# Two PSUM banks for the attention's projections, an earlier load of their weights, and another order of the prologue

## The reference

```python
def gdn_mixer(h, w_in, conv_w, a_log, dt_bias, out_norm, w_out):
    proj = h @ w_in                      # q, k, v | z | b | a
    ...
    beta = jax.nn.sigmoid(b)
    g = -jnp.exp(a_log) * jax.nn.softplus(a + dt_bias)
    o = gated_delta_rule_chunked(q, k, v, beta, g)
    ...
def mla_mixer(h, w_in, q_latent_norm, w_q_up, w_out, k_nope, k_rope, v, cos, sin):
    proj = h @ w_in
    c_q = rmsnorm(proj[..., :MLA_Q_RANK], q_latent_norm)
    z = proj[..., MLA_Q_RANK:]
    q = (c_q @ w_q_up).reshape(B, L, MLA_HEADS, MLA_QK)
    ...                                  # rope, causal softmax, times v
    return (o * jax.nn.silu(z)) @ w_out
```

## Time and profile before

| | us |
|---|---|
| median of 3 runs | 2503.44 (2501.28 to 2508.81) |
| the profiled execution's own time | 2494.57 |
| its span | 2492.8 |
| TensorE busy | 2286.7 (92%) |
| VectorE busy | 961.1 (39%) |
| ScalarE busy | 747.1 (30%) |
| mean granted clock | 0.951 |

### The profile page before, as it was taken

The page is one execution under the profiler, slowest core; times in us unless marked ns, Lnnn a source line. Parts: engine busy times, 40 slices in busy tenths (PEclk is TensorE's granted clock), DMA queues, the critical chain, the costliest instruction groups (busy, mean ns, idle before and its releaser), DMA issues.

```text
span 2492.8 us, 42870 instructions
## 1 busy us (share of the span) xinstructions
PE 2286.7 (92%) x19147; PEld 1651.8 (66%) x19147; DVE 961.1 (39%) x1821; ACT 747.1 (30%) x1376; POOL 0.2 (0%) x4
## 2 busy tenths in 40 slices
PE   4899999999998998788999999798999988999999
PEld 4678778878777687444444444356566546888888
DVE  1435535544544301222322220356226634556532
ACT  2434343343443201233433421442344422000000
POOL 0000000000000000000000000000000000000000
PEclk8899989989999799889998999899999998999999
DMA  4122222122121142111111112121110031433330
GB/s 160 35 69 71 68 69 70 52 87 70 52 70 52 49 118 68 30 30 30 30 46 57 37 34 68 55 70 36 35 34 1 1 101 34 131 85 89 94 101 26
DMA packets 200624, 150.41 MB, mean 60 GB/s; under 512 B 16360, under 2 KB 198122, under 8 KB 200058
## 3 DMA queue, kind: packets, MB, share of 16 engines
q1 hardware_dynamic: 200442, 147.69, 19.9%
HBM read 143.41 MB, written 4.26 MB: 59 GB/s over the span
## 4 chain that ended last, share of the span: by engine, by line
PE 85%; ACT 6%; DVE 5%; issue 3%; SPq 1%; DMA 1%; DVEq 0%; ACTq 0%
PE PS L2226 15%; PE PS L1505 11%; PE PS L1533 5%; PE PS L442 5%; PE PS L674 5%; PE PS L736 4%; PE PS L1286 3%; PE PS L1295 3%; PE PS L1288 3%; PE PS L1465 2%; PE PS L792 2%; PE PS L680 1%; PE PS L717 1%; PE PS L718 1%; PE PS L2347 1%
## 5 line engine op out<-in xcount | busy, mean ns | idle before, releaser
L2226 PE MATMUL PS<-hn_all,ring 128*128 128x264 f32 x1536 | 426.3, 414 | 2.5 <-DVE scr L2781 1.5
L2226 PEld LDWEIGHTS PS<-hn_all,ring 128*128 128x128 f32 x1536 | 292.5, 201 | 51.2 <-ACT scr L2551 1.9
L674 PE MATMUL PS<-hn_all,ring 128*128 128x512 f32 x256 | 117.0, 601 | 7.3 <-DMA ring<-in_mla_w_q_up 7.3
L442 PE MATMUL PS<-big,ring 128*128 128x264 f32 x512 | 115.8, 390 | 2.4 <-DMA ring<-in_gdn_w_out 2.4
L442 PEld LDWEIGHTS PS<-big,ring 128*128 128x128 f32 x512 | 98.3, 192 | 19.9 <-issue 2.7
L736 PE MATMUL PS<-big,ring 128*128 128x512 f32 x256 | 111.2, 592 | 0.0
L1286 PE MATMUL PS<-ring,hn_all 128*128 128x256 f32 x384 | 95.4, 403 | 2.5 <-ACT scr L1731 2.5
L1505 PE MATMUL PS<-scr 128*128 128x256 f32 x352 | 84.8, 384 | 4.6 <-DVE scr L1996 4.6
L674 PEld LDWEIGHTS PS<-hn_all,ring 128*128 128x128 f32 x256 | 48.2, 193 | 59.6 <-issue 47.5
L736 PEld LDWEIGHTS PS<-big,ring 128*128 128x128 f32 x256 | 48.2, 190 | 58.3 <-issue 57.7
L869 ACT ACTIVATE scr<-PS,scr 128x528 f32<-128x528 f32 (+1 forms) x64 | 34.6, 541 | 169.6 <-DVE scr L955 169.4
(11 more groups left out here) (471 smaller groups left out, 4043.1 us busy)
## 6 DMA issues: line engine op xcount, KB each, us to landing
ring<-in_w_mod SPq DMA_DIRECT2D x24, 1024.0 KB, 5.4
ring<-in_gdn_w_in SPq DMA_DIRECT2D x16, 1024.0 KB, 5.5
ring<-in_w_in SPq DMA_DIRECT2D x12, 1024.0 KB, 5.4
hn_all<-in_w_ffn_in SPq DMA_DIRECT2D x22, 512.0 KB, 5.3
ring<-in_w_ffn_in SPq DMA_DIRECT2D x22, 512.0 KB, 5.2
ring<-in_mla_w_in SPq DMA_DIRECT2D x9, 1024.0 KB, 5.5
ring<-in_gdn_w_in SPq DMA_DIRECT2D x16, 512.0 KB, 5.3
ring<-in_gdn_w_out SPq DMA_DIRECT2D x8, 1024.0 KB, 7.2
```

Of the source, the lines that this page charges most:

```text
L442: ins = nc.tensor.matmul(PS[:, 2 * (m % 2) + h, 0:x.stop - x.start], wslot(m % 4, P, 16)[:, k, :], src[:, k, x], start=(k == 0), stop=(k = ...
L674: ins = mm(o, wz_pair(p)[:, k, j * P:(j + 1) * P], hq[:, k, :], start=(k == 0), stop=(k == KD - 1))
L2226: ins = mm(o, wslot(slot_, 256)[:, k, m * P:(m + 1) * P], hn[:, k, b * HALF:(b + 1) * HALF], start=(k == 0), stop=(k == KD - 1))
```

## The change

Three things change. In the prologue the tokens are loaded and transposed ahead of the small vectors; `b` and `a` are computed with the 32 weight columns stationary and `hn` moving, one step as each block of `hn` is there, in four groups of 32 output partitions (L2229 after), and are folded and transposed into rows by six small matmuls (`gate_rows`); the projections start ahead of the gates, and the gates' work on TensorE, ScalarE and VectorE is put between them. In the first attention the weights of pair 0 are loaded once block 5 of the output product is done, and the latent's weights go to slots 2 and 3. The pieces alternate between banks 7 and 6, each waits only for the last eviction of its own bank, VectorE's rotation has a semaphore of its own, and the product with the values, which also uses bank 6, waits for the last piece there.

```diff
-    put("ident32", (i[:, None] % B32 == j[None, :]).astype(np.float32))
+    put("ident32", (np.arange(P)[:, None] % B32 == j[None, :]).astype(np.float32))
...
+        bap = scr[:, 14 * D + 512:14 * D + 512 + L]
...
+        def piece_bank(n):
+            h, kind = PIECES[n - 1]
+            if h == 0:
+                return 7 - (n - 1) % 2
+            return {"z": 7, "qn": 6, "qr": 7, "ka": 6, "kb": 7, "v0": 6, "v1": 7, "vm": 6}[kind]
+
+        def piece_before(n):
+            return max([k for k in range(1, n) if piece_bank(k) == piece_bank(n)], default=0)
...
         def mla_sp(sp):
-            sp.wait_ge(*up("gout", KD))
-            wd = t["kv_w_down"].rearrange("(k p) n -> p k n", p=P)
-            w = wslot(0, 256)
...
+            sp.wait_ge(*up("gout", 6))
+            weights(0)
+            sp.wait_ge(*up("gout", KD))
+            wd = t["kv_w_down"].rearrange("(k p) n -> p k n", p=P)
+            w = wslot(2, 256)
+            for o, src in ((w[:, :, 0:192], wd), (w[:, :, 192:224], wd[:, :, 160:192]), (w[:, :, 224:256], wd[:, :, P:160]),
+                           (wslot(3, 256), w_min[:, :, 0:256])):
+                sp.dma_start(o, src).then_inc(s["md_in"], 16)
+            sp.wait_ge(*up("md_mm", 4))
             weights(1)
-            sp.wait_ge(*up("md_mm", 4))
-            weights(0)
...
-                if n > 1 and part != 1:
-                    pe.wait_ge(*up("pev", n - 1))
-                o = PS[:, 7, :]
+                b_ = piece_bank(n)
+                last = piece_before(n)
+                if last and part != 1:
+                    if kind == "qn" and h >= 2:
+                        pe.wait_ge(*up("ogm", h - 1))
+                    elif PIECES[last - 1][1] == "qr":
+                        pe.wait_ge(*up("prot", evicted(last)[1]))
+                    else:
+                        pe.wait_ge(*up("pev", evicted(last)[0]))
+                o = PS[:, b_, :]
...
                     pe.wait_ge(*up("ogm", n))
+                if nxt:
+                    in6 = max(k for k, x in enumerate(PIECES) if x[0] == n + 1 and piece_bank(k + 1) == 6) + 1
+                    pe.wait_ge(*up("pev", evicted(in6)[0]))
...
-                V.tensor_tensor(qr_b[h % 2], PS[:, 7, :], rope[:, N_META:L], ALU.mult).then_inc(s["pev"], 1)
+                V.tensor_tensor(qr_b[h % 2], PS[:, piece_bank(piece_no(h, "qr")), :], rope[:, N_META:L], ALU.mult)\
+                    .then_inc(s["prot"], 1)
...
             sp.dma_start(CT[:, :], t["tables"]).then_inc(s["const_in"], 16)
+            sp.dma_start(min_, t["meta_tokens"]).then_inc(s["x_in"], 16)
+            for k in range(4):
+                sp.dma_start(xin[:, k, :], t["x"][0, k * P:(k + 1) * P, :]).then_inc(s["x_in"], 16)
...
-            sp.dma_start(min_, t["meta_tokens"]).then_inc(s["x_in"], 16)
...
+            pe.wait_ge(*up("vec_in", 16 * 24))
+            nc.tensor.transpose(PS[:, 0, 0:P], rows_a, ident)
...
-            pe.wait_ge(*up("hn0", 1))
-            for c in range(NCH):
-                for k in range(KD):
-                    ins = mm(PS[0:C, 0, 32 * c:32 * c + 32], hn[:, k, c * C:(c + 1) * C], wba[:, k, :],
-                             start=(k == 0), stop=(k == KD - 1))
+            for k in range(KD):
+                pe.wait_ge(*up("hn0", k + 1))
+                g = 32 * (k % 4)
+                for h in range(2):
+                    ins = mm(PS[g:g + 32, 4 + h, 0:HALF], wba[:, k, :], hn[:, k, h * HALF:(h + 1) * HALF], start=(k < 4),
+                             stop=(k >= 4))
             ins.then_inc(s["ba_mm"], 1)
...
+            def gate_rows():
+                pe.wait_ge(*up("act_g", 2))
+                pe.wait_ge(*up("vec_ev", 1))
+                for c in range(NCH):
+                    ins = mm(PS[0:C, 0, 32 * c:32 * c + 32], bap[:, c * C:(c + 1) * C], const("ident32"), start=True, stop=True)
+                ins.then_inc(s["ba_mm"], 1)
+
+            def gate_sums():
+                pe.wait_ge(*up("ba_ev", 1))
...
-            for name in ("qa", "qb", "ka", "kb", "v0a", "g0a", "g0b", "v0b", "g1a", "g1b"):
+            item("qa", 0)
+            gate_rows()
+            for name in ("qb", "ka"):
+                item(name, 0)
+            gate_sums()
+            for name in ("kb", "v0a", "g0a", "g0b", "v0b", "g1a", "g1b"):
                 item(name, 0)
...
-            for name in ("qa", "qb", "ka", "kb"):
-                raw(name, 0)
+            raw("qa", 0)
+            gates_a()
+            raw("qb", 0)
+            gates_b()
+            raw("ka", 0)
+            raw("kb", 0)
+            gates_c()
```

More of the change, by code:

```diff
@@ L167 @@
     "gla_r": ("ms0", 1), "gcopy": ("rev", 16), "gla_l": ("rr", 16), "lam_d": ("csil_z", 1),
-    "gsil": ("h_out", 16), "gfin": ("hn0", 1), "fs_d": ("mx", 64), "fp_d": ("pn", 64), "fv_d": ("pt", 64), "ft_d": ("tr", 64),
-    "op_d": ("sc", 64), "ov_d": ("ex", 64), "os_d": ("pj", 104), "ot_d": ("pev", 104), "lrl": ("rstd0", 1), "mo_t": ("go_t", 8),
+    "gsil": ("h_out", 16), "gfin": ("hn0", 8), "fs_d": ("mx", 64), "fp_d": ("pn", 64), "fv_d": ("pt", 64), "ft_d": ("tr", 64),
+    "op_d": ("sc", 64), "ov_d": ("ex", 64), "os_d": ("pj", 104), "ot_d": ("pev", 88), "prot": ("dve_g", 2), "lrl": ("rstd0", 1), "mo_t": ("go_t", 8),
 }
@@ L579, in piece_no, with evicted @@
             return PIECES.index((h, kind)) + 1
+        def evicted(n):
+            return n - sum(x[1] == "qr" for x in PIECES[:n]), sum(x[1] == "qr" for x in PIECES[:n])
+        def piece_bank(n):
[5 more added lines that the diff above has]
+            return max([k for k in range(1, n) if piece_bank(k) == piece_bank(n)], default=0)
         def last_piece(h):
@@ L744, in early @@
                     if m == 0:
-                        pe.wait_ge(*up("pev", len(PIECES)))
+                        pe.wait_ge(*up("pev", evicted(len(PIECES))[0]))
+                        pe.wait_ge(*up("prot", MLA_HEADS))
                     else:
@@ L751, in mla_pe @@
                 nxt = n + 1 < MLA_HEADS
-                pe.wait_ge(*up("pev", last_piece(n)))
+                pe.wait_ge(*up("pev", evicted(last_piece(n))[0]))
+                pe.wait_ge(*up("prot", n + 1))
                 score(n, 3)
@@ L846, in piece @@
                 act.wait_ge(*up("pj", piece_no(h, kind)))
+                b_ = piece_bank(piece_no(h, kind))
                 if kind == "z":
@@ L2101, in _ @@
             sp.dma_start(rows_c, t["gla_gate_bias_2"][0].rearrange("z (k p) -> (z k) p", p=P)).then_inc(s["vec_in"], 16)
-            sp.dma_start(min_, t["meta_tokens"]).then_inc(s["x_in"], 16)
-            for k in range(4):
-                sp.dma_start(xin[:, k, :], t["x"][0, k * P:(k + 1) * P, :]).then_inc(s["x_in"], 16)
             sp.dma_start(wba, w_gdn[:, :, GDN_BA:GDN_BA + 32]).then_inc(s["vec_in"], 16)
@@ L2482, in _ @@
                 A(sq0[:, k, :], hT[:, k, :], ACT.Square).then_inc(s["sq0_done"], 1)
-            act.wait_ge(*up("vec_ev", 1))
-            for n, name in enumerate(("c", "cctx")):
-                act.wait_ge(*up("csil_z", 1))
-                A(csil[:, n::32], cols(name), ACT.Silu).then_inc(s["c_act"], 1)
+            act.wait_ge(*up("vec_tr", 1))
+            A(vecs[:, 0:2 * P + 4], PS[:, 0, 0:2 * P + 4], ACT.Copy).then_inc(s["vec_ev"], 1)
             act.wait_ge(*up("ms0", 1))
@@ L2496, in _, with gates_a, gates_b, gates_c @@
             A(nega, alog, ACT.Exp).then_inc(s["act_g"], 1)
+            act.wait_ge(*up("vec_ev", 1))
+            for n, name in enumerate(("c", "cctx")):
+                act.wait_ge(*up("csil_z", 1))
+                A(csil[:, n::32], cols(name), ACT.Silu).then_inc(s["c_act"], 1)
             act.wait_ge(*up("ba_mm", 1))
-            A(g3[0], ba[:, :, 0:16], ACT.Exp, scale=-1.0).then_inc(s["act_g"], 1)
-            act.wait_ge(*up("dve_g", 1))
-            act_link(A(gx[3], gx[2], ACT.Exp))
-            A(gx[3], gx[3], ACT.Ln, bias=one[0:C]).then_inc(s["act_g"], 1)
-            act.wait_ge(*up("gate_gc", 1))
-            A(GV[:, 0:96], PS[0:C, 0, 0:96], ACT.Copy).then_inc(s["act_g"], 1)
-            A(gx[4], PS[0:C, 0, 0:96], ACT.Exp).then_inc(s["act_g"], 1)
-            act.wait_ge(*up("dve_g", 2))
-            A(gx[5], gx[5], ACT.Exp).then_inc(s["act_g"], 1)
+            A(two(bap), PS[:, 4:6, 0:HALF], ACT.Copy).then_inc(s["act_g"], 1)
+            def gates_a():
+                act.wait_ge(*up("ba_mm", 2))
+                A(g3[0], ba[:, :, 0:16], ACT.Exp, scale=-1.0).then_inc(s["act_g"], 1)
+            def gates_b():
+                act.wait_ge(*up("dve_g", 1))
+                act_link(A(gx[3], gx[2], ACT.Exp))
+                A(gx[3], gx[3], ACT.Ln, bias=one[0:C]).then_inc(s["act_g"], 1)
+            def gates_c():
+                act.wait_ge(*up("gate_gc", 1))
+                A(GV[:, 0:96], PS[0:C, 0, 0:96], ACT.Copy).then_inc(s["act_g"], 1)
+                A(gx[4], PS[0:C, 0, 0:96], ACT.Exp).then_inc(s["act_g"], 1)
+                act.wait_ge(*up("dve_g", 2))
```

(2 more changed lines are left out.)

50 lines of the change are left out of this document (20 added, 30 removed).

## The result

| | before | after |
|---|---|---|
| median, us | 2504.76 (2501.28 to 2508.81, 4 runs) | 2418.43 (2414.95 to 2422.33, 4 runs) |
| the profiled execution's own time | 2494.57 | 2422.33 |
| its span | 2492.8 | 2420.6 |
| TensorE busy | 2286.7 | 2265.0 |
| mean granted clock | 0.951 | 0.955 |

The ratio is 0.9656, 95% interval 0.9638 to 0.9674: 86.3 us by the medians, 72.2 by the two profiled executions. The forecast was 2427, within 2412 to 2455. Ratios are of the runs outside a slower state that a few executions fall into, so a ratio can differ by some tenths of a per cent from that of two medians.

The account below looks back on a forecast made before the run. TensorE fills 85% of the span, so gains lie where it idles or runs at half clock. 14.3 + 9.3 + 7.5 + 37 + 8 = 76.1 us; 76 off the runs' median 2503.44 gives 2427, range 2412 to 2455.

Parts of the forecast that it names:

- prologue, net: Prologue, measured by the start of `v0b`: 26.2 us gained less 11.9 given back, 14.3 us net, bounds 5 and 18.5.
- weights of pair 0: Start of the first attention: a 7.30 us DMA wait and 2.0 us of half clock in `z` go, 9.3 us.
- head 0's pieces: First attention: with two banks evictions lie beside the pieces, so the scores come sooner; 7.5 us taken.
- loop, waits of 15 iterations: Loop over heads: looser eviction waits gain 3.6 us in seven long iterations, 1.5 in eight short; 37 us.
- loop, clock: Loop over heads: half-clock stretches that follow the pieces' gaps mostly go; 8 us, bounds 0 and 9.1.
- Tokens first: Start of the prologue: `x` is issued earlier, so TensorE reaches the tokens at 12.0, 7.0 us earlier; bounds 5 to 8.
- the lower one: Prologue: lower bound, 0.9 us, for how far behind `hn` the matmuls of `b` and `a` end; 3.6 was taken.
- What is given back: Prologue, from `qa`'s end to `v0b`: gates now between projections cost 9.6 us, `v0b` at the half clock 2.3 more.
- The stall before `g0a`: Prologue, behind the projections: a sign that the forecast holds, a TensorE stall of about 4 us.
- That the prologue gives all back: Rival, 10%: gates, convolutions and SiLU become the prologue's chain; gain 0 to 5 us instead of 14, time 2438.
- That evictions bind the loop anyway: Rival, 5%: ScalarE's order holds each piece of the loop as before; gain 10 us there, time 2462.
- That many small waits make the clock fall in each iteration: Rival, 2%: two banks split the loop's waits into many small ones; 7 us lost, time 2510.

Follow-up runs that it names:

- e_balate: Kernel after, but the matmuls of `b` and `a` wait for all eight blocks of `hn`: 2416.59 us, ratio 0.9675.
- e_weights: Kernel before with only head pair 0's weights loaded earlier, during the output product: 2494.32 us, ratio 0.9978.
- e_banks: Kernel before with only the two alternating banks and their waits: 2445.60 us, ratio 0.9765.
- e_prologue: Kernel before with only the prologue's part of the change: 2480.19 us, ratio 0.9906.
- e_banks_serial: Kernel before with two banks, but each piece still waits for the eviction of the piece right in front: 2512.65 us, ratio 1.0054.
- e_vserial: Kernel after, but value pieces of heads behind the first wait for the eviction of the piece right in front: 2433.98 us, ratio 0.9755.
- e_zlate: Kernel after with head 0's first piece `z` put behind the norm's reductions: 2412.95 us, ratio 0.9666.
- both last edits: Kernel after with `z` behind the norm's reductions and the gates ahead of the raw keys: 2407.96 us, ratio 0.9644; run again 2405.03, 0.9615.

## Why the prediction was right, and where it was off

| step | predicted, us | by the profiles, us |
|---|---|---|
| prologue, net | 14.3 | 17.4 |
| weights of pair 0 | 9.3 | 9.3 |
| head 0's pieces | 7.5 | 7.3 |
| loop, waits of 15 iterations | 37 | 41.0 |
| loop, clock | 8 | 9.1 |
| all else | 0 | -11.9 |
| sum | 76.1 | 72.2 |

The terms that the change moves come to 84.1 us, 8 more than forecast, each of the right kind. That the two profiles differ by 72.2, close to the 76, is luck of the two executions; the medians, 86.3, fit the 84.1.

**Prologue.** Tokens first were sized at 7.0 us and gave 7.3. `b` and `a` were taken to end 3.6 us behind `hn`; they end 1.1 behind it. That is the term mis-sized here, by 2.5 us of the 3.1 that the prologue gained more: I held that four matmuls of one group in a row would overlap little, and `e_balate` shows 32 MATMULs of 264 columns, in that same order, in 3.73 us at a clock of 0.51, 0.12 us each. Of my bounds the lower one, from the earlier trace rows, was the right one to lean to. What is given back was forecast as 9.6 us up to `v0b` and 2.3 for its clock. Measured from the end of `qa`, `v0b` starts 26.5 us behind it for 17.3, so 9.2, and runs 2.15 longer. The stall before `g0a` is 3.58 us for "about 4".

**The start of the attention.** 7.30 of wait and 2.02 of clock went, as forecast, though the prediction's own subtraction, 9.05 - 6.9, is 2.15 and not 2.0. Two counts in it are wrong and change nothing, since its sum goes by columns: seven pieces stand behind `z`, not eight, and they are 22 MATMULs, not 24. Ln to first score takes 16.13 us for 23.41, 7.3 less. The two terms are not apart from each other. From L660 to the first score the weights alone (`e_weights`) gain 7.5 us, since 2 come back as half clock in the pieces, the banks alone (`e_banks`) 8.2, and the two together 16.8.

**The loop.** 24.0 and 21.4 were forecast, 23.93 and 21.00 measured: seven times 3.69 and seven times 1.90 are 39.1 us for 14 iterations, and the first one, from its first score to its product, gained 1.9 (17.80 us for 19.66): 41.0 where I had 37. The long iteration's terms, 4.9 + 1.3 + 0.1 - 0.5 from 9.33, give 3.5 and not 3.6. The short iteration gained more than I gave it, since its `kb` waits 0.1 us for the rotation and not 0.4. The falls of the clock, 9.1 us in this profile of before, went whole; `e_weights` has 3.4 us of them under the same waits, so that this term came out near its 8 is partly the luck of which profile was read.

**The rivals.** That the prologue gives all back: `e_prologue` has 23.5 us. That evictions bind the loop anyway: TensorE's idle time there is 5.5 us. That many small waits make the clock fall in each iteration: not here, but `e_banks_serial` shows that it is a real mechanism, 13.4 us in 14 iterations, where the waits stay as long as they were. What I had against it was half right: the freed waits do take the gaps away, but the clock had not fallen "after long value-making stretches". Two of the three falls of before stand at the end of a short iteration, and only the one from 1327 on lies among the values' pieces.

The Trainium skill (TensorE: Matmul & The Clock Gate, section HAM oscillation) had PSUM double-buffering without further gain; here it has a ratio of 0.9765. The page puts the idling of the kernel it starts from down to DMA waits, and tries the double-buffering once its loop has been rewritten against them. Here the idle time ended with evictions, and that row of the profile was what to go by.

**All else.** -11.9 us is the part that the sum did not have. 10.6 of it lie in the GDN layer behind `v0b`, where no instruction differs: from the first chunk's 32x32 products to the row behind the latent's product (L660, in the kernel after L676) it took 923.96 us in the profile of before (111.74 to 1035.70) and 934.59 in that of after (94.34 to 1028.93), with a granted clock of 0.94 and 0.92 in 145 to 830 us. Another 1.4 lie behind the loop, less 0.2 in which the terms above do not meet. Executions of one and the same instructions differ by more than that. With the old prologue the stretch is 924.0 in before, 927.2 in `e_banks_serial`, 927.8 in `e_weights` and 938.2 in `e_banks`; with the new one it is 934.6 and 927.9 in the two profiles of after, and from 921.7 (`e_vserial`) to 938.1 (`e_zlate`) in the others; `e_prologue` has 927.4, and its time gained more than its 17.4 us and not less. So it is chance of single executions for the most part. The profile of before was a quick one, 10 us under its median, that of after a slow one, 4 over, and the medians show 86.3 and not 72. Whether a small part is caused (the two profiles with both last edits have the longest, 945.0 and 942.7) stays open.

## What to carry to other kernels

Where a matmul waits for the eviction of the one in front, read the idle time and the granted clock of that stretch together: here a second bank with looser waits took both away, and a second bank alone took neither. A wait of 4 us on TensorE ahead of small matmuls cost its length and some 3 us more at the half clock behind it (`e_zlate`: 19.6 us for 26.7); independent matmuls that are already there (here `z`) belong into it. When two operands of a matmul can change places, count the MATMULs and not the moving columns alone: 96 of 32 columns were 14.29 us, 32 of 264 in four column groups, with more columns in sum, 3.73. And before a sum from one profile is held against a result, look how far two profiles of the same instructions lie apart: a sum can agree with one of them by luck.
